# Gathering both expert tables in turn with one index tile, and weighing the rows by pairs on ScalarE

## The reference

```
q = h2 @ w_q;  s1, s2 = q1 . keys[0], q2 . keys[1]        # 8 heads, 128 keys on either side
v1, i1 = top_k(s1, 16);  v2, i2 = top_k(s2, 16)
top_s, pos = top_k(v1[:, None] + v2[None, :], 16)          # 16 of 256 sums for each head
idx  = i1 * 128 + i2 at pos;  gate = softmax(top_s)
act  = gelu(sum_d expert_u[idx] * h2)                       # 128 experts for each token
out  = sum_k gate * act * expert_v[idx]
```

## Time and profile before

| | |
|---|---|
| median of 3 runs | 3206.51 us (3203.05 to 3211.17) |
| profiled execution: span from the first to the last instruction | 3215.5 us |
| GpSimd, 2048 gathers | 2245.9 us busy (1115.4 for U, 1130.5 for V) |
| VectorE | 2051.6 us busy, 1024 dots 1238.6 |
| TensorE | 2267.0 us busy, mix 1229.4 |
| ScalarE | 296.6 us busy |
| DMA | 1210.54 MB, mean 376 GB/s |

### The profile page before, as it was taken

One profiled execution on the slowest core, in us unless ns is written; L12 is line 12 of the kernel. 1 busy time (PEld: TensorE's weight loads), 2 busy tenths in 40 slices (PEclk: granted clock), 3 DMA queues, 4 the chain that ended last, 5 costly groups with the idle time before them and its releaser, 6 DMA issues.

```text
span 3215.5 us, 27380 instructions
## 1 busy us (share of the span) xinstructions
PE 2267.0 (71%) x9248; PEld 950.2 (30%) x9248; DVE 2051.6 (64%) x4962; ACT 296.6 (9%) x476; POOL 2249.6 (70%) x2062
## 2 busy tenths in 40 slices
PE   7877568878666588777765578887767665556666
PEld 5553323423233134223322224432322221111111
DVE  2588865666777855655788855666587776444441
ACT  1120001110000011111000000122000000000000
POOL 0246666787777776777777776778777777777775
PEclk9878779889778799989877788889988887787668
DMA  5799999999999999999999999999999999999998
GB/s 198 280 344 363 375 359 409 409 342 410 379 367 378 367 410 409 400 352 377 409 394 382 382 372 409 383 360 346 384 402 382 406 376 384 408 408 406 409 410 321
DMA packets 332348, 1210.54 MB, mean 376 GB/s; under 512 B 37040, under 2 KB 37168, under 8 KB 332208
## 3 DMA queue, kind: packets, MB, share of 16 engines
q0 software_dynamic: 294912, 1073.87, 86.5%
q1 hardware_dynamic: 37296, 134.91, 11.0%
HBM read 1204.44 MB, written 4.19 MB: 376 GB/s over the span
## 4 chain that ended last, share of the span: by engine, by line
POOL 35%; issue 12%; DVE 10%; DMA 7%; PE 6%; ACT 0%; POOLq 0%; DVEq 0%
POOL v_ring L436 18%; POOL u_ring L424 17%; DMA v_ring<-table_v,idx_v 5%; DVE u_ring L998 4%; DMA u_ring<-table_u,idx_u 3%; PE acc L632 2%; PE pt L462 2%; PE po L462 1%; DVE rc L867 1%; DVE rc L872 1%; DVE top_i L818 0%; DVE top_i L828 0%; DVE top_v L825 0%; DVE top_v L815 0%; DVE sum_p L853 0%
## 5 line engine op out<-in xcount | busy, mean ns | idle before, releaser
L998 DVE CUSTOM_DVE_ANT_0 u_ring<-u_ring,h2s 128x1024 f32<-128x1024 f32 x1024 | 1238.6, 1223 | 884.1 <-DMA u_ring<-table_u,idx_u 870.6
L632 PE MATMUL acc<-v_ring,wmask 128*32 128x512 f32 x4096 | 1229.4, 765 | 558.4 <-DMA v_ring<-table_v,idx_v 512.7
L424 POOL DMA_INDIRECT u_ring<-table_u,idx_u x1024 | 1115.4, 1089 | 604.5 <-issue 297.8
L436 POOL DMA_INDIRECT v_ring<-table_v,idx_v x1024 | 1130.5, 1104 | 349.4 <-issue 303.4
L632 PEld LDWEIGHTS acc<-v_ring,wmask 128*32 128x32 f32 x4096 | 220.7, 126 | 1435.9 <-DMA v_ring<-table_v,idx_v 1144.2
L462 PE MATMUL pt<-hT,w_ring 128*128 128x256 f32 (+1 forms) x1440 | 276.9, 350 | 10.5 <-DVE uT L911 9.9
L462 PEld LDWEIGHTS pt<-hT,w_ring 128*128 128x128 f32 x1440 | 237.1, 199 | 56.3 <-issue 32.8
L462 PE MATMUL po<-hT,w_ring 128*128 128x256 f32 (+1 forms) x800 | 158.2, 353 | 9.6 <-ACT kT L692 7.7
L462 PEld LDWEIGHTS po<-hT,w_ring 128*128 128x128 f32 x800 | 132.2, 198 | 38.7 <-issue 25.1
L618 PE MATMUL small<-ident,idx_f 128*32 128x32 f32 x256 | 13.5, 242 | 157.6 <-DVE idx_u L881 150.3
L451 PE MATMUL pt<-ident,rb 128*128 128x128 f32 x284 | 48.1, 321 | 68.2 <-ACT rb L667 42.2
(11 more groups left out here) (160 smaller groups left out, 1669.6 us busy)
## 6 DMA issues: line engine op xcount, KB each, us to landing
w_ring<-wstream SPq DMA_DIRECT2D x240, 512.0 KB, 6.8
u_ring<-table_u,idx_u POOLq DMA_INDIRECT x1024, 7.9
v_ring<-table_v,idx_v POOLq DMA_INDIRECT x1024, 7.9
xs<-x_in_dram SPq DMA_DIRECT2D x8, 512.0 KB, 8.3
y_out_dram<-xs SPq DMA_DIRECT2D x8, 512.0 KB, 6.6
g_all<-norm SPq DMA_DIRECT2D x1, 512.0 KB, 8.2
keysT<-keys SPq DMA_DIRECT2D x1, 128.0 KB, 7.2
chan_sb<-chan SPq DMA_DIRECT2D x1, 19.0 KB, 7.8
```

The costliest lines, as they stand in the source:

```text
L424: nc.gpsimd.indirect_dma_start(out=u_ring[:, k % U_SLOTS, :], out_offset=None, in_=peer_u, in_offset=bass.IndirectOffsetOnAxis(ap=idx_u[:, ...
L436: nc.gpsimd.indirect_dma_start(out=v_ring[:, slot, :], out_offset=None, in_=peer_v, in_offset=bass.IndirectOffsetOnAxis(ap=idx_v[:, b % ST ...
L632: mm = nc.tensor.matmul(acc[32 * i:32 * i + 32, half * 512:(half + 1) * 512], wmask[:, quarter % 2, i, 32 * j:32 * j + 32], v_ring[:, t % ...
L998: d = V.tensor_tensor_reduce(u, u, h2s[:, b % STASH, :], 1.0, 0.0, ALU.mult, ALU.add, dots[:, quarter % 2, at:at + 1])
```

## The change

U and V use the same index tile, and both are gathered in turn (U, V, U, V) into the two halves of one slot of 2048 floats; the ring has 8 such slots. A tile now holds 64 tokens x 2 heads: partitions 0 to 63 one head, 64 to 127 the next, for the tokens of one half of the block. A tick is one such tile, and two ticks (the two halves of the block) make a pair. GpSimd waits for `pair_done` of the pair four before, once in four gathers.

The normed input is kept as `h2r`, both halves of the tokens repeated over the upper and the lower 64 partitions; VectorE writes two quarters of it, ScalarE copies the other two (step `h2`). Indices and gates lie side by side in `turn_src` and are turned together (`turn_picks`); the gates' Exp and normalisation move ahead of that, so `look_up` now waits for the Exp. ScalarE makes for each tick a gate mask (`gate_mask`: the constant `stack`, two stacked identities of 64, times the turned gate) and, by pairs, Gelu of two dots and two weight masks of 128 x 64 (`weigh`). TensorE mixes each pair at the tick after it (`mix`): two tiles, each into 64 columns. VectorE's `weigh` and `place` are gone, as is the lag of V. The copies of q and k go to `rd` and `cvT`. In f=0 the first ranking's steps stand between the pieces of the PEER query, and `WHEN` has other numbers.

The diff, cut to its core:

```diff
-WHEN = [(-1, 8, 26, 42, 58), (0, 66, 74, 82, 90), (90, 240, 262, 284, 306), (308, 492, 516, 540, 564),
+WHEN = [(-1, 2, 20, 42, 62), (0, 70, 80, 90, 100), (100, 236, 266, 298, 328), (328, 488, 520, 552, 584),
...
-            for s in range(BLOCKS * GROUPS + V_LAG):
-                if s >= V_LAG:
-                    gather_v(s - V_LAG)
-                if s < BLOCKS * GROUPS:
-                    gather_u(s)
+            for t in range(TICKS):
+                b, q, i, r = place(t)
+                if t % QPICKS == 0:
+                    pool.wait_ge(idx_kept, picked(b, q))
+                if t % 2 == 0:
+                    wait(pool, pair_done, (t - SLOTS) // 2 + 1)
+                for table, lo, landed in ((peer_u, 0, u_in), (peer_v, D, v_in)):
+                    nc.gpsimd.indirect_dma_start(
+                        out=ring[:, t % SLOTS, lo:lo + D], out_offset=None, in_=table,
+                        in_offset=bass.IndirectOffsetOnAxis(ap=idx_t[:, b % STASH, q, i, r:r + 1], axis=0),
+                    ).then_inc(landed[t % SLOTS], 16)
...
+            def mix(p):
+                if p % PAIRS == 0:
+                    wait(pe, acc_free, p // PAIRS)
+                pe.wait_ge(wmask_ready, p + 1)
+                for half in range(2):
+                    for i in range(2):
+                        slot = (2 * p + i) % SLOTS
+                        if half == 0:
+                            pe.wait_ge(v_in[slot], 16 * ((2 * p + i) // SLOTS + 1))
+                        mm = nc.tensor.matmul(acc[HALF * i:HALF * i + HALF, half * 512:(half + 1) * 512],
+                                              wmask[:, slot, :],
+                                              ring[:, slot, D + half * 512:D + (half + 1) * 512],
+                                              start=(p % PAIRS == 0), stop=(p % PAIRS == PAIRS - 1))
+                mm.then_inc(pair_done, 1)
...
             for k in range(-1, END):
+                if k % 2 == 0 and 0 < k <= TICKS:
+                    mix(k // 2 - 1)
                 for step in STEPS.get(k, ()):
...
+            def gate_mask(p):
...
+                for t in (2 * p, 2 * p + 1):
+                    b, q, i, r = place(t)
+                    a = nc.scalar.activation(gmask[:, t % SLOTS, :], stack[:], copy,
+                                             scale=gate_t[:, b % STASH, q, i, r:r + 1])
+                a.then_inc(gmask_ready, 1)
+            def weigh(p):
+                lo = 2 * p % SLOTS
+                act.wait_ge(dots_done, p + 1)
+                nc.scalar.activation(acts[:, lo:lo + 2], dots[:, lo:lo + 2], ACT.Gelu).then_inc(gelu_done, 1)
+                act.wait_ge(gmask_ready, p + 1)
+                act.wait_ge(gelu_done, p + 1)
+                for slot in (lo, lo + 1):
+                    a = nc.scalar.activation(wmask[:, slot, :], gmask[:, slot, :], copy,
+                                             scale=acts[:, slot:slot + 1])
+                a.then_inc(wmask_ready, 1)
```

More of the change, by code:

```diff
@@ L153 @@
 TICKS = BLOCKS * PICKS
-END = TICKS + GROUP * (V_LAG + 2)
+END = TICKS + 2
 def picked(b, q):
@@ L602, in front @@
                     small_bank("picks")
-                    spread_out(pick_cols, idx_f).then_inc(idx_turned, 1)
-            small_uses = {"picks": 0, "weights": 0, "sums": 0}
+                    for h in range(2):
+                        for half in range(2):
+                            mm = nc.tensor.matmul(small[HALF * h:HALF * h + HALF, 32 * half:32 * half + 32],
+                                                  ident[:, HALF * half:HALF * half + HALF], turn_src[:, h, :],
+                                                  start=True, stop=True)
@@ L607, in small_bank @@
+                    mm.then_inc(idx_turned, 1)
+            small_uses = {"picks": 0, "sums": 0}
             def small_bank(what):
                 wait(pe, idx_kept, small_uses["picks"])
[L610 removed]
                 wait(pe, sum_kept, small_uses["sums"])
                 small_uses[what] += 1
[L614 to L619 removed]
@@ L964, in front @@
                     dve.wait_ge(invh_ready, b + 1)
-                    step(V.scalar_tensor_tensor(h2s[:, b % STASH, :], xs[:, b % X_SLOTS, :], invh[:, i:i + 1],
-                                                g2_all[:], ALU.mult, ALU.mult))
+                    for half in range(2):
+                        r = slice(HALF * half, HALF * half + HALF)
+                        last = V.scalar_tensor_tensor(h2r[r, b % H_SLOTS, half, :], xs[r, b % X_SLOTS, :],
+                                                      invh[r, i:i + 1], g2_all[r, :], ALU.mult, ALU.mult)
+                        if half == 0:
+                            step(last)
+                    last.then_inc(h2_ready, 1)
                 if name == "rank":
```

246 lines of the change are left out of this document (89 added, 157 removed).

## The result

The changed kernel takes 3681.19 us (median of 4 runs, 3675.87 to 3683.54) against 3208.84 us (4 runs) for the kernel before: a ratio of 1.147, 95% interval 1.145 to 1.149. A second measurement beside other kernels gives 1.145 (1.142 to 1.148). The forecast was 3247 us in a range of 3090 to 3390, so the time lies outside it, on the side of rival C.

A forecast was written before the change was run, and what follows sets the result against it. GpSimd was taken as one of two bounds, beside the DMA. Along GpSimd, 128 + 2527 + 420 + 169 + 12 = 3256, less 9 (trace span above median), gave 3247 us, 1.3% slower; range 3090 to 3390.

The forecast's parts named there:

- rival C: Ring runs dry: Gelu and masks wait behind the front's Sigmoids and scores, GpSimd stands; 3397 us, chance 0.15.
- own gathers and "issue": GpSimd's own work: 2048 gathers at 0.94 + 0.294 us as before, 2527 us, no change.
- Waits: GpSimd's waits behind the first gather: from 234 us, -16 at the start and -49 for longer stretch, about 169.
- The longer chain behind a slot: U slots now wait for the mix, 8 to 9.3 us in all: 0 in the calm, up to +150 us.
- Start: +6: First gather waits for Exp and the turned index: 128 us instead of 122, other end 132.
- Lag ticks: -30: U and V together, 36 lag ticks gone at the end, first ticks fuller: -30 us, from -46 to +5.
- Stretch: +99: Gathers that start beside a dot wait for it; dots now come singly: 0.41 us each, 420 us, up from 321.
- harmless rhythm: Gather pairs every 2.56 us or near, a released gather waiting only 0.08 us for each dot.
- slow rhythm of 3.2 us: Where GpSimd is the bound, a U gather starts inside a dot: pair period 3.2 us, stretch 0.72 for each dot.
- ScalarE, TensorE: no bound: ScalarE busy 1013 of 3200 us; TensorE's mixing 970 to 1700 us, under 5.12 us for each pair.
- A: The even rhythm wins and the DMA is the bound: 3117 us, faster, chance 0.31.
- B: No change: stretch 0.31 as before, waits 218; 3197 us, or 3205 to 3215 with lost slack, chance 0.12.

The follow-up runs named there:

- kernel with the early Exp: Changed kernel with V gathered and mixed 12 ticks after U, weighing a pair later, first ranking's Exp one piece group earlier: 3195.5 us, 0.995 of before.
- quickest version: Kernel with V lag of 12 ticks and earlier first Exp, plus mix and weighing behind the front's steps of their tick: 3179.4 us, 0.991 of before.

## Why the prediction was wrong, point by point

**The sum by its own terms**, along GpSimd, predicted and measured:

| term | predicted | measured |
|---|---|---|
| first gather at | 128 | 134.5 |
| own gathers and "issue" | 2527 | 1925 + 553 = 2478 |
| stretch | 420 | 302 |
| waits behind the first gather | 169 | 752 |
| end | 12 | 15 |
| sum | 3256 | 3682 |

**Waits, the step that failed.** The term stood at 169 us and measured 752. The step behind it: "each front step of VectorE that wants a product of its own tick now waits for the mix ahead of it, some 3 us. I count some 125 such steps, 375 us of VectorE's idle time ... and hide them there". The coupling was seen, and it was wrong to hide it in VectorE's idle time. The 3 us were the mix's own products; but a mix first stands for its masks, those for the dots, and the dots for such a step of the front. That is a circle, and it has no idle time of its own to hide in: what a step waits is passed on. VectorE's waits for the other two engines rose by 663 us, and they made the dots late. Putting mix and weigh behind the front took 347 of its 901 us away and 6.7 points of time, and a pair of ticks between weigh and mix in place of that, with V's lag, brought them to 378 us and the time to 1.002. The same holds for "*The longer chain behind a slot*": I held the latency of a slot (8 to 9.3 us) against the slack of the ring, taking the dot as done when V lands. The slot experiments show that this chain is not the price: freeing U with its dot gives 1.146, ten slots for V 1.149, and the kernel that holds each slot a pair longer 0.992.

**Start: +6, it was +12.** The order of the steps was right, the time of ScalarE's turn was not:

```profile
129.28 0.69 ACT L718 ACTIVATE h2r<-pz,invh 128x512 f32<-128x512 f32 x1 [0.58 <-PE pz L464]
129.99 1.28 ACT L728 ACT_TABLE_LOAD   x1
131.28 0.23 ACT L728 ACTIVATE turn_src<-turn_src 128x32 f32<-128x32 f32 x1
...
134.01 0.18 DVE L989 CAST idx_t<-small 128x32 uint32<-128x32 f32 x1
...
134.48 1.95 POOL L433 DMA_INDIRECT ring<-table_u,idx_t  x1 [131.59 <-DVE idx_t L989]
```

Exp's table load starts at 129.99, not 123.7: ScalarE has the third key scores (the first row) behind it only at 129.97. Both ends I had put (128 and 132) were passed. The kernel with the early Exp waits 127.4 us for its index and not 131.6 here, 4 of the 12 us back.

**Lag ticks: -30.** From 134 to 361 us the DMA moves 368 GB/s (357 before), and GpSimd waits 59.0 us for the mix there, where I had put 56 for dots. The size agrees, but the wait is another one than I had in mind, so that is in part luck; no run prices the 36 lag ticks by themselves.

**Stretch: +99, it was -19.** (1.086 + 1.089 - 2 x 0.94) x 1024 = 302 us. The sign was wrong. In the quiet stage, the only place where I looked for it, the harmless rhythm is there: the pair comes every 2.56 us with the dot 0.22 us behind V's start (the stage that answers to the earlier trace rows):

```profile
3399.28 0.94 POOL L433 DMA_INDIRECT ring<-table_v,idx_t  x1 [0.30 <-issue]
3399.50 1.23 DVE L1001 CUSTOM_DVE_ANT_0 ring<-ring,h2r 128x1024 f32<-128x1024 f32 x1 [1.33 <-DMA ring<-table_u,idx_t]
...
3400.52 1.01 POOL L433 DMA_INDIRECT ring<-table_u,idx_t  x1 [0.30 <-issue]
...
3401.84 0.93 POOL L433 DMA_INDIRECT ring<-table_v,idx_t  x1 [0.30 <-issue]
...
3403.08 1.00 POOL L433 DMA_INDIRECT ring<-table_u,idx_t  x1 [0.31 <-issue]
```

The "harmless" 0.08 for each dot is the 1.01 of U against 0.94. The mean I took for the mixed stages supposed that GpSimd stays the bound there. It was not, since it stood for the mix; that this is why the gathers met fewer dots is argued, not shown. In the quickest version, where it stands less, the stretch is (1.125 + 1.077 - 1.88) x 1024 = 330 us. So there too the slow rhythm of 3.2 us (0.72 for each dot, 737 us) did not last. The Trainium skill ("SBUF — State Buffer", section "Who interferes with whom") says that a VectorE instruction with two SBUF inputs contends with a GpSimd instruction that reads SBUF, and that issue order decides who blocks. The gathers agree again, and not beside dots alone; a scan of the front holds one back for 2 us:

```profile
2638.76 2.28 DVE L805 TENSOR_TENSOR_SCAN hT<-hT 128x1024 f32<-128x1024 f32 x1
2638.81 2.97 POOL L433 DMA_INDIRECT ring<-table_v,idx_t  x1 [0.30 <-issue]
```

The dots, whose mean is 1223 ns before and after the change, show no waiting on their side.

**ScalarE, TensorE: no bound.** ScalarE is busy 1063.5 us for 1013 predicted; the masks of 128x64 take 0.33 to 0.34 and not 0.23 each (594 us busy in place of 471, as they overlap a little), and the rest came out 72 us smaller. TensorE's mix is 1386 us, in the middle of 970 to 1700. That neither is full was right and was no evidence: order, not work, set the time. Table loads: 145 as read from the order, and in the timeline Exp starts 1.29 us behind its load's start (131.28 - 129.99). The drain that the Trainium skill has at a switch ("ScalarE: Activation LUTs", section "What ACT_TABLE_LOAD costs") could only lie ahead of the load, and there the gap is 0.02 us: by that page 2.66 us for each switch, by these rows 1.3.

**Rivals.** A (DMA the bound, 3117) did not happen here; with the distance between weigh and mix and a lag of 12 the kernel comes to 3179. B did not happen. C had the sign and the criterion right ("Waits ... over 300 with DMA under 370 GB/s"), 752 us at a mean of 329 GB/s, but its price was 75 places of 2 us at the switches of ScalarE; with 133 of the 145 table loads gone the loss is still 12.2 of 14.7 points. C named the masks behind the front's work as the reason, and not the way back, from a late mix over the front to the dots; so it had half of the mechanism.

## What to carry to other kernels

Between engines that work in program order, a consumer placed in the same step as its producer makes every step behind it wait for the whole chain in front of it; follow such a chain until it closes on itself before hiding its cost in idle time. Put a step of distance there, and first where the engine that waits has the most independent work behind the wait: a pair of ticks between masks and mix took the whole loss of 14 points back, without one more mask or slot where transfers are slow (0.992), and with V's lag of two ticks and two masks more elsewhere (1.002); one between dots and masks took half of it back. Within a step, the engine's own independent work goes ahead of what may have to wait.

## What the runs showed of the hardware that was not expected

The same kernel of before took 3209 to 3217 us on most devices and 3362 and 3397 us on two. The kernel with the mix alone a pair later shows on one of these what differs: its quiet stage, first, beside the one of the quickest version on a device of the other kind (core time, busy of each engine, clock, DMA share, GB/s):

```profile
3000.00:3300.00 300.00, 159.49 (x422) 34.65 (x418) 130.31 (x211) 65.91 (x260) 217.46 (x211) 0.71 0.97 368
```

```profile
2700.00:3000.00 300.00, 184.70 (x464) 41.33 (x463) 144.22 (x233) 73.53 (x291) 228.65 (x235) 0.94 1.03 409
```

DMA share is 0.97 with 368 GB/s there, 1.03 with 409 here. The Trainium skill ("DMA: Bandwidth & Descriptors", section "Measured (HBM→SBUF, 128 partitions, SWDGE, issued from GpSimd)") says that a core gets about 358 GB/s when the other core of its HBM domain streams too. Whether that was so in these runs, no trace shows. And a small one: ScalarE's copy of 128x64 with a scale read from SBUF takes 334 to 340 ns, while the Gelu of 128x2 takes 200.

What stays open: what the kernel with its mix alone a pair later takes where before takes 3210 us; and whether the changed kernel with its mix alone a pair later and behind the front's steps, without any lag of V, would do as well as the version with the lag; it was not tried.
